# A two-layer encoder step on one core: four-quadrant merges, three-part scores, half steps spread, the group norm in two parts

## The reference

```python
def step(Sm, inp):                                   # mixer B, 4 heads of 64
    r_t, w_t, k_t, v_t, kk_t, a_t = inp
    sa = jnp.einsum('bhij,bhj->bhi', Sm, kk_t)
    Sm = (Sm * w_t[:, :, None, :] - sa[..., None] * (kk_t * a_t)[:, :, None, :]
          + v_t[..., None] * k_t[:, :, None, :])
    return Sm, jnp.einsum('bhij,bhj->bhi', Sm, r_t)
...
mu = jnp.mean(y, axis=-1, keepdims=True)
var = jnp.mean(jnp.square(y - mu), axis=-1, keepdims=True)
y = ((y - mu) * lax.rsqrt(var + GN_EPS)).reshape(B, S, RW_WIDTH) * P['rw_gn_w'] + P['rw_gn_b']
y = (y + bonus.reshape(B, S, RW_WIDTH)) * g
...
s = (jnp.einsum('bqhc,bkc->bhqk', qlb, ckv)          # mixer C, keys of chunks up to the query's
     + jnp.einsum('bqhr,bkr->bhqk', qrb, kr)).astype(jnp.float32) * MLA_SCALE
pr = jax.nn.softmax(s, axis=-1).astype(ckv.dtype)
...
y = jnp.concatenate([y_rg, y_rw, y_mla], axis=-1) @ P['w_out']
return x + y, ...
```

## Time and profile before

| | |
|---|---|
| median of three runs | 1990.3 us |
| the profiled execution | 1981.6 us |
| its span, first to last instruction | 1979.8 us |
| TensorE busy in the span | 95% |
| VectorE, ScalarE, GpSimd busy | 50%, 36%, 5% |
| mean granted TensorE clock | 0.971 |

### The profile page before, as it was taken

One profiled execution on the slowest core, in us unless ns is written; L12 is line 12 of the kernel. 1 busy time (PEld: TensorE's weight loads), 2 busy tenths in 40 slices (PEclk: granted clock), 3 DMA queues, 4 the chain that ended last, 5 costly groups with the idle time before them and its releaser, 6 DMA issues.

```text
span 1979.8 us, 37383 instructions
## 1 busy us (share of the span) xinstructions
PE 1885.3 (95%) x16458; PEld 1727.7 (87%) x16458; DVE 989.2 (50%) x1693; ACT 710.3 (36%) x1270; POOL 94.3 (5%) x100
## 2 busy tenths in 40 slices
PE   6998998999999999999999799989998999999997
PEld 5975885899789999999999478759986999999997
DVE  6676455454335544344367755455443455353533
ACT  4444444553334222122345344453533332121212
POOL 2000000200010000000100000001000200000001
PEclk9998999999999999999999799979998999999998
DMA  5210001453022222222222000013610222222221
GB/s 219 69 40 1 4 2 45 153 171 118 33 64 83 89 86 86 97 82 89 86 75 75 8 3 3 4 55 137 214 54 22 75 90 92 86 87 85 96 86 56
DMA packets 38593, 149.51 MB, mean 76 GB/s; under 512 B 4384, under 2 KB 4544, under 8 KB 36768
## 3 DMA queue, kind: packets, MB, share of 16 engines
q1 hardware_dynamic: 36288, 131.05, 19.6%
q0 software_dynamic: 2144, 16.06, 2.1%
HBM read 139.68 MB, written 7.41 MB: 74 GB/s over the span
## 4 chain that ended last, share of the span: by engine, by line
PE 89%; DVE 5%; ACT 4%; issue 1%; POOL 1%; DMA 0%; DVEq 0%; SPq 0%; ACTq 0%; POOLq 0%
PE PS L525 80%; PE PS L645 8%; PE PS L859 1%; ACT hH L984 1%; POOL sq L461 1%; DVE stat L1671 0%; ACT aP L984 0%; PE PS L953 0%; ACT L984 0%; DVE wL L1362 0%; POOL msq L503 0%; ACT sq L984 0%; DVE hL L1371 0%; DVE kf L1538 0%; ACT wH L984 0%
## 5 line engine op out<-in xcount | busy, mean ns | idle before, releaser
L525 PE MATMUL PS<-hH,wH 128*128 128x272 f32 x2272 | 486.4, 296 | 31.0 <-DMA cst<-cst_in 16.7
L525 PE MATMUL PS<-hH,wL 128*128 128x272 f32 x2272 | 475.4, 290 | 0.0
L525 PE MATMUL PS<-hL,wH 128*128 128x272 f32 x2272 | 474.7, 291 | 0.0
L1362 DVE TENSOR_TENSOR wL<-ring,wH 128x1024 fp32r<-128x1024 f32 x238 | 301.0, 1266 | 215.7 <-ACT wH L984 215.4
L525 PEld LDWEIGHTS PS<-hH,wH 128*128 128x128 f32 x2272 | 359.7, 190 | 42.9 <-issue 19.1
L984 ACT ACTIVATE wH<-ring 128x1024 fp32r<-128x1024 f32 x238 | 249.6, 1051 | 333.5 <-PE PS L525 332.1
L525 PEld LDWEIGHTS PS<-hH,wL 128*128 128x128 f32 x2272 | 361.1, 190 | 0.0
L525 PEld LDWEIGHTS PS<-hL,wH 128*128 128x128 f32 x2272 | 358.8, 190 | 0.0
L525 PE MATMUL PS<-hidH,wL 128*128 128x272 f32 x1024 | 212.0, 288 | 0.0
L525 PE MATMUL PS<-hidH,wH 128*128 128x272 f32 x1024 | 211.7, 288 | 0.0
L525 PE MATMUL PS<-hidL,wH 128*128 128x272 f32 x1024 | 211.1, 288 | 0.0
(11 more groups left out here) (279 smaller groups left out, 2468.1 us busy)
## 6 DMA issues: line engine op xcount, KB each, us to landing
ring<-wall SPq DMA_DIRECT2D x238, 512.0 KB, 3.3
lw<-lw_in POOLq DMA_DIRECT2D x2, 2240.0 KB, 9.6
xT<-x_in SPq DMA_DIRECT2D x4, 544.0 KB, 7.1
y_out<-hT SPq DMA_DIRECT2D x8, 272.0 KB, 2.1
mem<-mem_in POOLq DMA_DIRECT2D x2, 1024.0 KB, 5.2
mks<-mks_in POOLq DMA_DIRECT2D x2, 1024.0 KB, 9.0
mvs<-mvs_in POOLq DMA_DIRECT2D x2, 1024.0 KB, 11.7
memk_out<-mkp POOLq DMA_DIRECT2D x2, 1024.0 KB, 5.3
```

The source lines that it names most:

```text
L525: return e.matmul(out, lhsT=a, rhs=b, start=start, stop=stop)
L1362: tt(wL[:, n % SPLIT], ring[:, n % RING], plain(wH[:, n % SPLIT]), ALU.subtract).then_inc(w_lo, 1)
```

## The change

1. **Merges in four quadrants.** The masked matrix `P` is now kept with the two chunks swapped in the partitions, the merge's first sum is written to bank 2x and its second to bank 2x+1, so that the four products of a merge step (two chunks, two sums) lie in four different quadrants. The starting identity is four products of 256 columns instead of two of 512. `cross` writes to bank 7, shared by both lanes, and waits for the cross before it to be masked.
2. **Three-part scores and queries.** Queries, keys, `cq` and the query weights are split into high parts and remainders; each score and each query product becomes three fast ones. Queries come in two pieces of 272 columns instead of 256, 256 and 32. This adds roundings on ScalarE (`queries_hi`, `uq_hi`) and subtractions on VectorE (`queries_lo`, `keys_lo`, `rotary_keys_lo`, `uq_lo`). The split parts lie in ring slots of "out" tiles 0 to 2, whose loads now wait, and in memory that `mem32` takes later, whose load waits for the last score. The mask rows are copied by GpSimd (`marks`).
3. **Half steps.** `weigh(u-2)` moves to the first half step, `turn(u-1)` to the second. `TURNS` has 8 half steps beside the factor steps and 18 beside group 4 as before, then 49 beside the rest of the recurrence, 8 beside and after the group norm. Scores have bank 4; projections, `weigh` and the early norm share bank 5.
4. **The group norm in two parts.** Positions 0 to 255 are normed at units 29 to 36, the other 288 after the recurrence.
5. **Rows of "out"** are split and multiplied in the order 0, 1, 4, 5, 6, 7, 2, 3; five of them are rounded before the last half steps.

The core of the diff; twelve leading blanks and empty lines are taken off:

```diff
 UNITS = [(h, b) for h in range(HEADS) for b in range(5)]
-PIECES = [(0, 256), (256, 512), (512, T)]
-USES = [("v", j) for j in range(5)] + [("p", 3), ("p", 4), ("v", 5), ("v", 6), ("p", 0), ("p", 1), ("p", 2)]
+NORM_PARTS = [(0, 2 * GRP), (2 * GRP, T)]
+NORM_UNITS = (29, 34, 35)
+OUT_ROWS = (0, 1, 4, 5, 6, 7, 2, 3)
+PIECES = [(0, T // 2), (T // 2, T), (0, SEQ), (SEQ, KEYS)]
+USES = [("v", j) for j in range(7)] + [("p", p) for p in (2, 3, 0, 1)]
+FIRST = len(USES)
 for _u, (_h, _b) in enumerate(UNITS):
-    USES.append(("s", _u))
-    if _h + 1 < HEADS:
-        USES.append(("p", 5 * (_h + 1) + _b))
+    USES += [("s", _u)] + [("w", _u - 2)] * (_u > 1)
+    if _h + 1 < HEADS and _b < 4:
+        USES.append(("p", 4 * (_h + 1) + _b))
+    if _u in NORM_UNITS:
+        USES.append(("g", NORM_UNITS.index(_u)))
+USES += [("w", len(UNITS) - 2), ("w", len(UNITS) - 1)]
...
-    return order + "a" * (ATT_STEPS - order.count("a"))
+    for i in range(ALONE):
+        order += "r" + (BESIDE_FACTORS[i] if i < FACTOR_STEPS else "a" * (1 + i % 2))
+    pairs, left = (len(REC_STEPS) - ALONE + 1) // 2, ATT_STEPS - order.count("a") - len("".join(BESIDE_NORM))
+    for j in range(pairs):
+        order += "r" * min(2, len(REC_STEPS) - order.count("r")) + "a" * (left * (j + 1) // pairs - left * j // pairs)
+    for beside in BESIDE_NORM:
+        order += "r" + beside
+    return order
...
+elif kind == "w":
+    e.wait_ge(s["a_o"], at(l, "a_o", n + 1))
+elif kind == "g":
+    name = ("gn_mean", "gn_var", "gn_gated")[n]
+    e.wait_ge(s[name], at(l, name))
...
+    l, (st, i) = n // NT, STREAM[n % NT]
+    if st == "out" and i < 2:
+        e.wait_ge(s["q_mm"], at(l, "q_mm", 2 * HEADS))
+    elif st == "out" and i == 2:
+        e.wait_ge(s["a_score"], at(l, "a_score", 5 * (HEADS - 1)))
...
+    e.wait_ge(s["rw_y"], at(l, "rw_y", 2))
+    e.wait_ge(s["a_score"], at(l, "a_score", len(UNITS)))
     e.dma_start(mem32, mem_d).then_inc(tokens_ld, 16)
...
+        if nth("cross", g, b) > 1:
+            e.wait_ge(s["cross_out"], at(l, "cross_out", nth("cross", g, b) - 1))
...
+            for c in range(2):
+                q = rows_of[1 - c]
+                unit = ident[q, CH * (1 - c):CH * (1 - c) + CH], bc(C("id64", 0, CH, q), 4)
+                part(pair(bank(2 * x, 0, 256), 4)[rows_of[c]], *unit)
+                part(pair(bank(2 * x + 1, 0, 256), 4)[q], *unit)
             for c in chunks_of(g):
-                r = rows_of[c]
-                unit = ident[r, CH * c:CH * c + CH]
-                part(pair(bank(2 * x), 8)[r], unit, bc(C("id64", 0, CH, r), 8))
-                part(bank(2 * x, 0, 256)[r, :], unit, P[x][r].rearrange("p a b -> p (a b)"), False)
+                q = rows_of[1 - c]
+                part(bank(2 * x, 0, 256)[rows_of[c], :], ident[q, CH * (1 - c):CH * (1 - c) + CH],
+                     P[x][q].rearrange("p a b -> p (a b)"), False)
         else:
             e.wait_ge(s["cross_out"], at(l, "cross_out", nth("cross", g, b)))
         for w in range(4):
             for c in chunks_of(g):
-                r = rows_of[c]
+                r, q = rows_of[c], rows_of[1 - c]
                 if 0 < b < levels_of(g) - 1:
-                    part(bank(2 * x, 64 * w, 64 * w + 64)[r, :], XX[x][r, 1, w, :], P[x][r, w, :], False)
-                last = part(bank(2 * x, 256 + 64 * w, 320 + 64 * w)[r, :], P[x][r, w, :],
-                            XX[x][r, 1, w, :] if b else C("id64", 0, CH, r), False)
+                    part(bank(2 * x, 64 * w, 64 * w + 64)[r, :], XX[x][q, 1, w, :], P[x][q, w, :], False)
+                last = part(bank(2 * x + 1, 64 * w, 64 * w + 64)[q, :], P[x][q, w, :],
+                            XX[x][q, 1, w, :] if b else C("id64", 0, CH, q), False)
...
+    def norm_early(i):
+        (norm_sum, norm_squares, norm_gate)[i](0)
...
-            halves(Q(t), bones, yrw[:, t, 0:T]).then_inc(s["gn_sum"], 1)
+        norm_sum(1)
+        norm_gate(1)
         yield
-        e.wait_ge(s["gn_sq"], at(l, "gn_sq"))
-        for t in range(2):
-            halves(Q(t), bones, ell[:, t, 0:T]).then_inc(s["gn_sum"], 1)
+        norm_squares(1)
...
-                last = mm(o[:, 0:b - a], W("uq", (k * HEADS + h) * 128, (k * HEADS + h + 1) * 128),
-                          cq[:, k, a:b], k == 0, k == 1)
+                last = three(mm, o[:, 0:b - a], [uqH(l, h)[:, k, :], uq(lwL, h)[:, k, :]],
+                             [cqH(l, k)[:, a:b], cqL[:, k, a:b]], k == 0, k == 1)
...
+        mm(o, aqH[rows, j, q], akH[rows, j, keys], True, False)
+        mm(o, aqH[0:QKD, j, q], akL(l, j)[0:QKD, keys], False, False)
+        mm(o, aqL[0:QKD, j, q], akH[0:QKD, j, keys], False, True).then_inc(s["a_score"], 1)
...
         for u, (h, b) in enumerate(UNITS):
             score(u)
+            if u >= 2:
+                weigh(u - 2)
+            yield
+            if h + 1 < HEADS and b < 4:
+                project(4 * (h + 1) + b)
+            if u in NORM_UNITS:
+                norm_early(NORM_UNITS.index(u))
             if u:
                 turn(u - 1)
-            yield
-            if h + 1 < HEADS:
-                project(5 * (h + 1) + b)
-            if u >= 2:
-                weigh(u - 2)
             yield
...
+        e.wait_ge(s["gn_sum"], at(l, "gn_sum", 4))
+        link(act(norm_rstd(1), norm_sums(1), ACT.Ln, scale=1.0 / 64, bias=K(C_GN)))
+        act(norm_rstd(1), norm_rstd(1), ACT.Exp, scale=-0.5).then_inc(s["gn_rstd"], 1)
+        yield
+        split(tile_no(l, "out", 1))
+        for k in OUT_ROWS[:5]:
+            if k > 3:
+                e.wait_ge(s["a_o"], at(l, "a_o", 10 * (k - 3)))
+            mixed_hi(hT if k >= 2 else rgo, k)
...
+                head_out(u - 2)
             e.wait_ge(s["a_max"], at(l, "a_max", u + 1))
             act(aP[0:n, u % 2, 0:nk], bank(bank_of(("s", u)), 0, nk)[0:n, :], ACT.Exp, scale=MLA_SCALE,
                 bias=stat[0:n, 18 + u % 2:19 + u % 2],
                 accum_out=stat[0:n, 20 + u % 2:21 + u % 2]).then_inc(s["a_exp"], 1)
+            yield
+            if u in (NORM_UNITS[0] + 1, NORM_UNITS[1] + 1):
+                norm_early(1 if u == NORM_UNITS[0] + 1 else 2)
+            if u == NORM_UNITS[1]:
+                sums_kept()
+            if h + 1 < HEADS and b in (1, 2):
+                queries_hi(4 * (h + 1) + b - 1)
+            if h + 1 < HEADS and b in (2, 3):
+                keys_hi(4 * (h + 1) + b)
             if u:
                 turned_out(u - 1)
-            yield
-            if h + 1 < HEADS:
-                (nope_out if b < 3 else keys_out)(5 * (h + 1) + b)
-            if u >= 2:
-                head_out(u - 2)
+            if h + 2 < HEADS and b == 3:
+                uq_hi(h + 2)
...
+    def norm_gated(i):
+        cols = slice(*NORM_PARTS[i])
+        e.wait_ge(s["gn_sq"], at(l, "gn_sq", i + 1))
+        e.wait_ge(s["g_out"], at(l, "g_out", i + 1))
+        for t in range(2):
+            gated = norm_sums(i, 1)[:, t, :]
+            stt(yrw[:, t, cols], yrw[:, t, cols], V(l, "gn_w", t), gated, ALU.mult, ALU.mult)
+            ins = stt(bonus[:, t, cols], bonus[:, t, cols], V(l, "gn_b", t), gated, ALU.add, ALU.mult)
+        ins.then_inc(s["gn_gated"], 1)
+        e.wait_ge(s["gn_gated"], at(l, "gn_gated", i + 1))
+    def norm_end(i):
+        y = yrw[:, :, slice(*NORM_PARTS[i])]
+        e.wait_ge(s["gn_rstd"], at(l, "gn_rstd", i + 1))
+        link(tt(y, y, norm_rstd(i), ALU.mult))
+        tt(y, y, bonus[:, :, slice(*NORM_PARTS[i])], ALU.add).then_inc(s["rw_y"], 1)
...
+        tt(aqL[0:QKD, h % 2, a:b], hT[0:QKD, h % 2, a:b], plain(aqH[0:QKD, h % 2, a:b]),
+           ALU.subtract).then_inc(s["q_out"], 1)
...
+        rotary_keys_lo(0)
+        keys_lo(2)
+        keys_lo(3)
+        queries_out(0)
+        yield
+        queries_out(1)
+        queries_lo(0)
+        yield
         for u, (h, b) in enumerate(UNITS):
+            if u == 0:
+                queries_lo(1)
             maximum(u, "a", *size(b), MLA_SCALE, bank_of(("s", u)))```

On TensorE, at the end of layer 0's recurrence, before: after the last state product (S and XX of lane 1, not shown) stand the score of unit 30, a turn, and the first sums of the group norm.

```order
L525 MATMUL PS<-ak_75,aq_74 128x128
L862 MATMUL PS<-cst_55,aP_76 32x32
L864 MATMUL PS<-cst_55,aP_76 128x32 x2
L525 MATMUL PS<-hT_50,cst_55 128x272 x4
L525 MATMUL PS<-cq_66,lw_52 128x256 x2
L525 MATMUL PS<-aPT_77,av_78 64x128 x4
L525 MATMUL PS<-ak_75,aq_74 128x256
L859 MATMUL PS<-cst_55,aP_76 128x128
L525 MATMUL PS<-cq_66,lw_52 128x256 x2
L525 MATMUL PS<-aPT_77,av_78 64x32 x3
L525 MATMUL PS<-ell_72,cst_55 128x272 x4
```

355 lines of the change are left out of this document (224 added, 131 removed).

## The result

The changed kernel takes 1974.9 us (median of five runs, 1970.8 to 1976.7), the kernel before 1990.3 (1984.9 to 1991.3); the ratio is 0.9937, 95% interval 0.9915 to 0.9960. The profiled executions lie closer together: 1976.2 us (span 1974.4) after, 1981.6 before.

A forecast was written before the change was run, and what follows sets the result against it. The prediction took TensorE as the bound beside the recurrence, VectorE in the factor steps, and attention round trips at the end. Terms summed to -20.9 us a layer, -41.8 for two, giving 1948.5 us, range 1922 to 1980.

The forecast's parts named there:

- merges: Recurrence merges and starting identity: four quadrants take a middle merge from 0.94 to 0.47 us; -11.2 us a layer.
- scores: Attention scores on TensorE: three fast products instead of one full-precision product save 1.2 us a head.
- queries: Query projection on TensorE: twelve fast products, 1.56 us, replace pieces of 2.7 us; 1.1 us saved a head.
- eleven half steps: Attention half steps moved beside the recurrence (49 for 38), 0.97 us each after the saving; +10.7 us a layer.
- early norm, six products: The early group norm brings six TensorE products of 256 columns at 0.53 us; +3.2 us a layer.
- factor steps: Start of the mixing stage: decays start 5 us late, at about 147.5, behind the first exponential; +3.3 us a layer.
- waits beside the recurrence: New waits of `weigh`, `cross` and scores beside the recurrence; +6 us a layer, bounds 0 and 16.
- the end: Last stretch before "out": 42.2 us becomes 24, including 2 for the lower clock; -18.2 us a layer, bounds 17 and 31.
- msq: Sum over the memory tokens right after tile 1 of "out": costed at 0, at most 4 us, in layer 0.
- lockstep rival: Beside the recurrence, the shared bank makes one serial chain, about 5.5 us a unit; 2020 us, chance 0.07.
- merge rival: Merges keep their price, by the bank rule or issue; 11.2 us a layer missing, 1971 us, chance 0.08.
- round-trip rival: Round trips through other engines hold TensorE up more than allowed, 16 us a layer; 1968.5 us, chance 0.15.

The follow-up runs named there:

- merges_two: The changed kernel with each merge's left half written to the same partition half as its right, so two quadrants work instead of four; 1994.7 us, ratio 1.0046.
- scores_full: The changed kernel with each score as one full-precision product on the same operands, remainder products left out; 1973.6 us, ratio 0.9942.
- tail_none: The changed kernel with all half steps of the attention beside the recurrence, none beside or after the group norm's second part; 1959.3 us, ratio 0.9867.
- norm_sooner: The changed kernel with the early group norm's three pieces at units 24, 29 and 34 instead of 29, 34 and 35; 1967.1 us, ratio 0.9909.
- rows_early: tail_none with the first weight split and five row roundings of "out" on ScalarE ahead of the last state product, remainders between norm steps; 1964.5 us, ratio 0.9896.
- spread_alone: The kernel before with only eleven more half steps of the attention beside the recurrence (49 for 38); 1984.5 us, ratio 1.0003.
- no_remainders: The changed kernel with full-precision scores on unrounded queries and keys, and all subtractions for their remainders gone; 1968.1 us, ratio 0.9908.
- rows_ahead: rows_early with three of the five early roundings behind the last turned block, and the memory tokens' load not waiting for the norm's end; 1956.6 us, ratio 0.9868.
- the nine fillers: Nine products nobody reads, put into TensorE's waits late in the memory attention and ahead of `mo`; on the changed kernel 1964.5 us, ratio 0.9894.

## Why the prediction was wrong

Direction and bounds held (1974.9 lies in 1922 to 1980); the size was off by 26 us. Per layer, in the prediction's own order, each change counted in TensorE's busy time and the waits in a row of their own:

| term | predicted | measured | from |
|---|---|---|---|
| merges | -11.2 | -10.1 and -9.0 undone; whole-kernel 21.6 for two | `merges_two` |
| scores | -7.7 (1.2 x 6.4 heads) | -0.6 | rows above, `scores_full` |
| queries | -7.0 | -6.0 (0.94 x 6.4) | rows above |
| eleven half steps | +10.7 | +9.5 (0.87 each) | `tail_none`'s eight |
| early norm, six products | +3.2 | +2.1 for four; two fell into the end | 0.53 each |
| factor steps | +3.3 | +4.7 | 27.0 to 31.7 |
| waits beside the recurrence | +6 | +5.2 (2.0 to 7.2 of idle time) | stretches 2 and 3 |
| the end | -18.2 | -9.7 | 42.2 to 32.5 |
| all | -20.9 | -4.7 and -4.5 | stretches |

The measured rows add up to -4.9 with merges at -10.1, and to -3.8 with -9.0. In stretches 2 and 3 they give TensorE 5.1 or 4.0 us less busy time, and the rows show 4.9 less (152.51 to 147.63).

- **The scores' rate is the step that failed first.** "I take 1.2, near the rate of the nearest row" carried the rate of 272 columns to scores of 128 to 512. A fast product of 128 columns starts no faster than every 0.11 us, so three of them cost more than the one they replace (0.48 for 0.42). The wide ones did not come out at that rate either: three passes over 512 columns would be 0.73 us by it, and took 0.90, for 0.97 before. Also, the five scores of before cost 3.3 us a head and not the 3.55 that I read off the chain. The lower bound that I gave myself, 0.2 a head, was near in number by luck: it had the 128-column score at 1.26 us and the others at the fast rate. `scores_full` shows it: 1973.6 without the scores' three parts, 1974.9 with them.
- **The end: the round trips were followed with one item in the wrong place.** I put one Ln and Exp with their table loads there; there are two. Unit 35's exponential is the first of the last stretch, and the early norm's Ln and Exp stand right behind it (318.48 to 322.44, 4 us). `norm_sooner` gives 2.6 of them back. I also allowed 2 us for the lower clock: the norm's three groups of 288-column products take 2.26 to 2.29 us each here, and two of them 1.23 and 1.24 in `rows_early`, where the clock is up. The five roundings ahead of the turned block of unit 37, which I had counted as ScalarE's time, are also TensorE's wait of 3.12 us. Only the 2.6 us rest on a run of their own; the rest is read from the rows, and no run takes it apart.
- **Half steps.** Their price was taken as 0.97, after a saving on scores that did not come, and is 0.87 of TensorE's busy time in `tail_none`, whose eight are of the last head and have no projection: near in size, in part by luck. With the waits that come with them, which the forecast had as a term of its own, a half step costs 1.19 in the kernel before (`spread_alone`) and 1.34 here.
- **Factor steps.** The mechanism was right and its size too small: 147.5 was forecast for the decays, and they start at 147.85 in a stage that began 1.7 us earlier, so 2 us later than forecast; `be` follows at 153.11. `no_remainders` shows that the remainders' subtractions are its cause: without them group 4 starts 4.2 us earlier.
- **Queries** are 1.0 short of the forecast, and some of what came is due to the dropped 32-column pieces: by the estimate above 0.4 of the 0.94 us a head.
- **Merges and new waits** came out near the forecast (-9.0 to -10.1 for -11.2, +5.2 for +6). The rival by which products from different row tiles cannot write one bank at once is refuted for different partitions: a merge of 32 records takes 0.52 to 0.64 us instead of 0.98 to 1.08, and undoing it costs 21.6 us. The Trainium skill (TensorEngine Tiling (Array Packing), Restrictions and Gotchas) states that rule without this limit; the measurement decides.
- **A term that I did not have: the rest of the program.** I added a saving to a span and took all else as fixed. The mixing stage saved 4.6 and 4.4 us here, and the memory attention and `mo` took 3.0 and 1.4 of them back. Between kernels of this study the memory attention alone varied by 4.1 us (106.9 to 111.0) with the same instructions. `msq`, which I costed at 0, did cost nothing here, but 4.9 us as soon as "out" began earlier (`rows_early`), and 2.1 in `rows_ahead`.

The lockstep rival did not come: 67 half steps beside the recurrence took 154.8 us, 4.6 a unit. The merge rival (1971) is nearest in number, and the round-trip rival (1968.5) next, but neither is what happened: `merges_two` refutes the one, and the other wanted 16 us of waits beside the recurrence, where 5.2 were added.

Per layer the two large misses, scores (7.1) and end (8.5), make 15.6 of the 16.2 us by which the mixing stage was off; the small ones nearly cancel. What stays open is the mixing stage's own spread of 0.2 to 4.2 us between kernels that differ only behind it (with and without the nine fillers).

## What to carry to other kernels

Splitting a full-precision product into three rounded ones paid little for single products: scores of 128 to 512 columns changed by -0.09 to +0.06 us each. The query projection, six products of 272 columns in a row, fell by a third (2.68 to 1.74 us a head), in part because a narrow piece was dropped. Price each width from a row of that width, and where there is none, take the bound and not the nearest row. Where work is moved out of a tail of round trips, moving part of it shifts the time (four half steps: 7.8 for 7.8), and moving all of it removes the round trips (eight: 15.9 for 10.7). Where TensorE waits often and briefly, a useless product shorter than the wait can be worth more than a saved one; one as long as the wait costs.
